# Block attention of a three-block model: rotated halves of q and k moved by transfers instead of matmuls, and one output piece placed before the last scores

## The reference, cut to what matters

```python
def apply_rope(t, cos, sin):
    t1, t2 = jnp.split(t, 2, axis=-1)
    return jnp.concatenate([t1 * cos - t2 * sin, t2 * cos + t1 * sin], axis=-1)

def moba_attention(x, w_qkv, w_o):
    qkv = (x @ w_qkv).reshape(B, T, 3, H, Dh)
    q, k, v = [jnp.transpose(qkv[:, :, n], (0, 2, 1, 3)).astype(f32) for n in range(3)]
    q = apply_rope(q, cos, sin) * (Dh ** -0.5)
    k = apply_rope(k, cos, sin)
    ...
    p = jax.nn.softmax(jnp.where(causal, q @ k.T, -jnp.inf), axis=-1)
    return (p @ v) @ w_o
```

## Time and profile before

| | |
|---|---|
| median of 3 runs | 1288.44 us (1288.23 to 1289.37) |
| the profiled execution | 1289.13 us, its span 1287.3 us |
| TensorE busy | 1240.8 us, 96% of the span |
| VectorE, ScalarE, GpSimd busy | 900.3, 640.5, 69.9 us |
| moved from and to HBM | 202.83 MB read, 158 GB/s over the span |

### The profile page before, as it was taken

How to read it: one execution, slowest core, us unless ns; L and a number is a source line. 1 busy time by engine, 2 the same in 40 slices (tenths; PEclk the granted TensorE clock), 3 DMA queues, 4 the chain that set the end, 5 groups by cost and what they waited for, 6 DMA issues and landing times.

```text
span 1287.3 us, 22080 instructions
## 1 busy us (share of the span) xinstructions
PE 1240.8 (96%) x9364; PEld 1086.4 (84%) x9364; DVE 900.3 (70%) x1433; ACT 640.5 (50%) x966; POOL 69.9 (5%) x43
## 2 busy tenths in 40 slices
PE   6999999999999999999999999999999999999997
PEld 4888898888888898778888889999898987788886
DVE  7456886767556677666765568989999766666555
ACT  3443446554445545555455545344455556655553
POOL 0022000002000061000100010000000000000000
PEclk8999999999999999999999999999999999999999
DMA  9442202775655373427565546455534443355550
GB/s 323 142 138 79 88 3 73 231 239 182 202 184 181 132 242 135 131 72 242 182 201 188 194 136 210 132 174 186 164 132 164 136 159 115 117 204 189 193 180 33
DMA packets 156355, 206.36 MB, mean 160 GB/s; under 512 B 9952, under 2 KB 129888, under 8 KB 156128
## 3 DMA queue, kind: packets, MB, share of 16 engines
q1 hardware_dynamic: 156256, 204.94, 48.3%
HBM read 202.83 MB, written 1.05 MB: 158 GB/s over the span
## 4 chain that ended last, share of the span: by engine, by line
PE 71%; DVE 19%; ACT 7%; issue 2%; DMA 0%; DVEq 0%; SPq 0%; ACTq 0%
PE PS L599 15%; PE PS L551 11%; PE PS L552 11%; PE PS L553 11%; PE PS L604 8%; DVE WW L2189 6%; PE PS L972 4%; DVE PH L2792 4%; ACT WW L1543 2%; PE PS L903 1%; DVE PA L2435 1%; ACT Xb L1582 1%; PE PS L943 1%; PE PS L676 1%; DVE PH L2810 1%
## 5 line engine op out<-in xcount | busy, mean ns | idle before, releaser
L2189 DVE TENSOR_TENSOR WW<-RG,WW 128x2048 fp32r<-128x2048 f32 x164 | 381.1, 2338 | 141.2 <-ACT WW L1543 141.0
L1543 ACT ACTIVATE WW<-RG 128x2048 fp32r<-128x2048 f32 x164 | 311.2, 1906 | 25.1 <-PE PS L553 24.5
L599 PE MATMUL PS<-AHL,WW 128*128 128x512 f32 x864 | 216.9, 392 | 0.5 <-DVE WW L2189 0.5
L551 PE MATMUL PS<-AHL,WW 128*128 128x256 f32 x704 | 203.3, 289 | 2.5 <-DVE AHL L2235 1.8
L552 PE MATMUL PS<-AHL,WW 128*128 128x256 f32 x704 | 199.1, 283 | 0.0
L553 PE MATMUL PS<-AHL,WW 128*128 128x256 f32 x704 | 199.1, 283 | 0.0
L599 PEld LDWEIGHTS PS<-AHL,WW 128*128 128x128 f32 x864 | 157.0, 189 | 30.0 <-DVE WW L2189 0.9
L551 PEld LDWEIGHTS PS<-AHL,WW 128*128 128x128 f32 x704 | 134.9, 192 | 5.3 <-issue 3.7
L552 PEld LDWEIGHTS PS<-AHL,WW 128*128 128x128 f32 x704 | 135.0, 192 | 1.7 <-issue 1.4
L553 PEld LDWEIGHTS PS<-AHL,WW 128*128 128x128 f32 x704 | 134.9, 192 | 0.0
L604 PEld LDWEIGHTS PS<-AHL,WW 128*128 128x128 f32 x864 | 118.4, 190 | 8.8
(11 more groups left out here) (375 smaller groups left out, 1829.0 us busy)
## 6 DMA issues: line engine op xcount, KB each, us to landing
RG<-in_ffn_w_in SPq DMA_DIRECT2D x44, 1024.0 KB, 5.3
RG<-in_w_ff SPq DMA_DIRECT2D x32, 1024.0 KB, 5.5
RG<-in_w_in SPq DMA_DIRECT2D x30, 1024.0 KB, 5.2
RG<-in_ffn_w_down SPq DMA_DIRECT2D x22, 1024.0 KB, 4.9
RG<-in_w_rkv SPq DMA_DIRECT2D x12, 1024.0 KB, 6.5
RG<-in_moba_w_qkv SPq DMA_DIRECT2D x12, 1024.0 KB, 6.5
RG<-in_w_o SPq DMA_DIRECT2D x4, 1024.0 KB, 7.9
RG<-in_wx_kv SPq DMA_DIRECT2D x4, 1024.0 KB, 5.4
```

The source lines that it names most:

```text
L551: e.matmul(o, lh, rh, start=start, stop=False)
L599: e.matmul(PS[b][:, :].rearrange("p (a t) -> p a t", a=2), wh, AHL[:, :, k * 256:k * 256 + 256], start=k == 0, stop=False)
L1543: s.activation(WH[hi_n % NW], ring(SPLIT[hi_n]), ACT.Copy, bias=0.0, scale=1.0).then_inc(s_hi, 1)
L2189: v.tensor_tensor(WL[lo_n % NW], ring(SPLIT[lo_n]), WH[lo_n % NW].bitcast(F32), ALU.subtract).then_inc(s_lo, 1)
```

## The change

The product with the permutation matrix is gone. In its place SP issues four transfers of 32 partitions by 512 columns (64 KB each) from `raw` to a new place `rot` in the tile `Xb`, swapped in pairs of 32 partitions (`rotate`). They stand in SP's list between the weights: `rotate(0)` behind mv3s, 1 behind mq3, 2 behind mk3s, 3 to 5 behind mo0 to mo2, 6 and 7 behind the first two pieces of the next feed-forward layer. The sign has moved into the table of sines. VectorE waits for the four transfers of a half (a count of 64 for each use) and reads `rot`. TensorE's waits before q and k pieces that write the PSUM banks again are now on `s_rw` instead of `s_rp`. Two waits are added on ScalarE. Lastly the output piece `moba_out(0, 1)` stands inside the step of heads 12 and 13, before their scores.

```diff
-               ('sel2', 2), ('pad', 14), ('perm', 128), ('cmask', 384), ('c01', 384), ('cos', 256), ('sin', 256)]:
+               ('sel2', 2), ('pad', 14), ('cmask', 384), ('c01', 384), ('cos', 256), ('sin', 256)]:
...
-    put('sin', np.tile(np.sin(ang), (4, 1)))
+    put('sin', np.where(p64 < 32, -1.0, 1.0) * np.tile(np.sin(ang), (4, 1)))
...
+        rot = [Xb[:, 1024 + 512 * n:1536 + 512 * n] for n in range(2)]
...
+            def rotate(u):
+
+                d.wait_ge(s_rw, u + 1)
+                for o_, i_ in ((0, 32), (32, 0), (64, 96), (96, 64)):
+                    d.dma_start(rot[u % 2][o_:o_ + 32, :], raw[u % 2][i_:i_ + 32, :]).then_inc(s_rot[u % 2], 16)
...
                             piece(f'f{f}{un}{j}', wcols(w_in, u * 256 * n + 256 * j, 256))
+                            if (f, j) == (1, 0):
+                                rotate(6 + u)
...
                     piece('mv3s', wcols(M, 2560, 512, 4, 4))
-                piece(f'mq{j}', wcols(M, 256 * j, 256))
-                piece(f'mk{j}s', wcols(M, 1024 + 256 * j, 256))
+                    rotate(0)
+                for u in range(2):
+                    piece(f'mk{j}s' if u else f'mq{j}', wcols(M, 1024 * u + 256 * j, 256))
+                    if j == 3:
+                        rotate(1 + u)
             for n in range(4):
                 piece(f'mo{n}', wcols(a['moba_w_o'], 512 * (n % 2), 512, 4 * (n // 2), 4))
+                if n < 3:
+                    rotate(3 + n)
...
                 if i in (12, 14):
+                    if between is not None:
+                        between()
                     e.wait_ge(s_rp, 8)
                     scores()
...
                     if u >= 4:
-                        e.wait_ge(s_rp, u - 3)
+                        e.wait_ge(s_rw, u - 3)
...
             moba_out(0, 0, (0, 1))
-            rope_turn(7)
+            e.wait_ge(s_rw, 8)
             moba_out(0, 0, (2, 3))
-            step()
-            moba_out(0, 1)
+            step(lambda: moba_out(0, 1))
...
+                if u == 0:
+                    s.wait_ge(s_tl, H_AT['ln1'] + 4)
                 s.activation(raw[u % 2], PS[4 + u % 4][:, :], ACT.Copy, bias=0.0, scale=1.0).then_inc(s_rw, 1)
...
             s.wait_ge(s_oa, 6)
+            s.wait_ge(s_rp, 8)
             rounded(OTf, (2,), 1.0, XH)
...
-                v.wait_ge(s_pm, u + 1)
-                own_dve(v.tensor_tensor(d_, PS[4 + u % 4][:, :].rearrange("p (m t) -> p m t", m=2), sinb, ALU.mult))
+                v.wait_ge(s_rot[u % 2], 64 * (u // 2) + 64)
+                own_dve(v.tensor_tensor(d_, rot[u % 2].rearrange("p (m t) -> p m t", m=2), sinb, ALU.mult))
```

More of the change, by code:

```diff
@@ L58, in constants @@
     put('sel2', (p // 64) == np.arange(2)[None, :])
-    n_out, n_in = f % 64, p % 64
-    same = (p // 64) == (f // 64)
-    put('perm', np.where(same & (n_out < 32) & (n_in == n_out + 32), -1.0, 0.0)
-        + np.where(same & (n_out >= 32) & (n_in == n_out - 32), 1.0, 0.0))
     t1 = np.arange(256)[None, :] - 128
@@ L214, in build @@
         s_fg, s_fx, s_fhh, s_fhl, s_dn = (sem(n) for n in ("ffn_gate", "ffn_prod", "ffn_hi", "ffn_lo", "ffn_down_mm"))
-        s_rw, s_rc, s_pm, s_rp, s_v2 = (sem(n) for n in ("rope_raw", "rope_cos", "rope_mm", "rope_out", "moba_v"))
+        s_rw, s_rc, s_rp, s_v2 = (sem(n) for n in ("rope_raw", "rope_cos", "rope_out", "moba_v"))
+        s_rot = [sem(f"rope_rotated{n}_in") for n in range(2)]
         s_sc, s_mx, s_ex, s_pn, s_pt, s_pta, s_pv, s_oa = (sem(n) for n in (
@@ L791, in attention, with attention_pairs @@
                     t.then_inc(s_pv, 1)
-            def attention_pairs(i):
+            def attention_pairs(i, between=None):
                 A = A1
@@ L1262, in tensor_program, with step @@
             mem_unit(3)
-            def rope_turn(u):
-                e.wait_ge(s_rw, u + 1)
-                e.matmul(PS[4 + u % 4][:, :], cst('perm'), raw[u % 2], start=True, stop=True).then_inc(s_pm, 1)
-            def step():
+            def step(between=None):
                 nonlocal heads
@@ L1272, in step @@
                     e.wait_ge(s_rp, heads // 2 + 2)
-                attention_pairs(heads)
+                attention_pairs(heads, between)
                 heads += 1
@@ L1287, in tensor_program @@
                     token_piece('mv3s', 6, 0, 1)
-                    rope_turn(5)
                     token_piece('mv3s', 7, 1, 1)
@@ L1305, in tensor_program @@
                         step()
-                        if u != 6:
-                            rope_turn(u - 1)
                     chan_piece(name, 4 + u % 4, 1)
@@ L1310, in tensor_program @@
                         step()
-                    elif u:
-                        rope_turn(u - 1)
             def moba_out(n, tt, ks=range(4)):
```

## The result

The changed kernel is slower. Four executions took 1299.12, 1299.17, 1300.71 and 6461.05 us. The last is an outlier that the comparison leaves out; the median of the other three, 1299.17 (1299.94 with it), stands for the kernel from here on. Runs of the kernel before beside them: 1288.84 (1288.23 to 1289.37). The ratio is 1.0083, with a 95% interval from 1.0070 to 1.0097. The forecast was 1295.0 with a range of 1287.5 to 1299.5: slower, as forecast, but by 10.3 us instead of 6.6. The one median lies just inside the range, the one of all four executions just outside.

The account below looks back on a forecast made before the run. It took TensorE as the bound, with VectorE close behind. Late rotations, carried through the loop and last heads, left the stage 6.65 us late; added to the median 1288.44 this gave 1295.0 us, range 1287.5 to 1299.5.

Parts of the forecast that it names:

- The queue: SP's full queue: transfers of rotations 0 and 1 stand behind 1 MB weights, landing at about 478.55 and 482.85.
- Rival B: SP's queue: small transfers do not queue behind the weights, rotation 1 is ready as before; 1287.7 us, chance 0.12.
- The sine product from SBUF: VectorE's product with the sines, reading SBUF instead of PSUM: 0.7 us taken against 0.68, no change.
- The clock: Behind TensorE's 7.7 us wait before the first score pair: half clock, mostly hidden; value 0.5 us, bounds 0 and 3.1.
- two waits of about 2 us: TensorE at the next two score pairs: waits about 2 us each, held by VectorE's and ScalarE's loop, 7.4 us late.
- The wait at the first output piece: TensorE's 1.17 us wait there grows by rotation 6's saved 0.85 us.
- First output piece: TensorE reaches it at 533.75 + 6.55 = 540.3, the 6.55 us lateness carried from the v pieces.
- Rotation 7 in at 543.55: Last rotation: raw half ready at 539.45, four transfers add 4.1 us; 7.3 us later than read before.
- head 12 to the last remainder 11.8: VectorE's last heads: between 10.6 and 13.0 us, 11.8 taken, against 12.97 before.
- Head 12 itself: VectorE's start on head 12, after TensorE's scores and the moved output piece: 548.3, 7.85 us later than 540.46.
- The end of the stage: End of mo3's remainder: 562.4 against 555.71, 6.65 us late, with nothing changed from there on.
- up to 2.6 more: Unknown size of the half-clock loss: up to 2.6 us beyond the value taken.

Follow-up runs that it names:

- 12: Changed kernel with rotations 0 to 2 earlier in SP's list, old output order, cosine product on VectorE, four filler matmuls: 1291.76 us, ratio 1.0023.
- 15: Changed kernel with rotations 0 to 5 re-placed in SP's list, old output order, cosine product on VectorE, four filler matmuls: 1287.73 us, ratio 0.9991.
- kernel 8: Changed kernel plus thirteen filler matmuls, results never read, in TensorE's waits, nine of them before the first score pair: 1297.82 us, ratio 1.0065.
- Experiment 4: Kernel before with the eight rotation matmuls left out and nothing in their place, so the result lacks the rotation: 1289.69 us, ratio 1.0005.
- kernel 5: Kernel before without any rotation, plus six filler matmuls, results never read, in TensorE's waits: 1287.15 us, ratio 0.9988.
- 13: Changed kernel with only SP's list changed, rotations 0 to 5 placed elsewhere among the weights: 1292.25 us, ratio 1.0021.
- 3: Kernel before with only the second output piece moved ahead of the scores of heads 12 and 13: 1289.98 us, ratio 1.0008.
- 14: Changed kernel with rotations 0 to 5 re-placed in SP's list, six filler matmuls and the old output order: 1288.86 us, ratio 1.0000.
- kernel 2: Changed kernel with halves 0 and 1 rotated by permutation matmul again, halves 2 to 7 by transfers: 1293.17 us, ratio 1.0032.
- kernel 10: Changed kernel with only rotations 0, 1 and 2 moved, to ahead of mq2, behind mk2s and behind mv2s: 1292.77 us, ratio 1.0030.
- 9: Changed kernel with halves 0 and 1 by matmul, rotation 2 ahead of mq3, six filler matmuls, old output order: 1288.03 us, ratio 0.9993.
- 6: Changed kernel with halves 0 and 1 by matmul and rotation 2 issued ahead of mq3 and mk3s: 1292.18 us, ratio 1.0023.
- 1: Changed kernel with SP's list reordered, rotation 0 ahead of mv2s and rotation 1 ahead of mv3s: 1296.31 us, ratio 1.0060.
- 7: Changed kernel with halves 0 and 1 by matmul, rotation 2 ahead of mq3 and mk3s, plus six filler matmuls: 1288.76 us, ratio 1.0001.
- 11: Changed kernel with rotations 0 to 2 earlier in SP's list, six filler matmuls and the old output order: 1292.66 us, ratio 1.0027.

## Why the prediction was right in direction and too small

All times here are those of the changed kernel plus 0.72, to stand beside before.

- **The queue: right.** Rotation 0 in at 479.2 (forecast 478.55), rotation 1 at 483.1 (482.85), landing 8.4 to 10.1 and 6.7 to 10.3 us after issue behind mv3s and mq3. Rival B's overtaking didn't come.
- **The sine product from SBUF, "I take 0.7, no change": wrong.** It took 1.39 us at rotation 1. With the 0.3 of the later landing the sum was ready at 485.3, not 484.3, and the first pair 7.0 late, not 6.0. The reason for the 0.7 is GpSimd's cosine product, below; without it (kernels 12 and 15) all eight sine products took 0.68 to 0.69. At the fifth pair 0.5 of this was left (7.0 late, forecast 6.55).
- **The clock, "value 0.5": too small by itself, and in the wrong place.** The forecast looked for it behind the first wait. There it was longer than taken (10.24 us, 5.12 of it over work) and hidden, as argued: of the two waits of about 2 us that were forecast for the pairs behind, the half clock used up the first (TensorE doesn't wait at the third pair) and left 1.61 of the second, where kernel 8 at full clock has 1.51 and 1.37. The forecast put nothing on a second window. The wait at the first output piece, which it made 1.17 + 0.85 = 2.0 us long itself, came out at 3.13, 1.07 of it by VectorE's remainder, with the clock at half for 3.42 behind it. From that piece to head 12 it cost 1.45 (9.47 us instead of 8.0); kernel 8, without the window, is 1.38 faster there.
- **First output piece: 541.9 instead of 540.3.** 0.5 is the rest from the first pair, 1.07 that VectorE's 512-column remainder stood still beside GpSimd's product. The forecast had "6.55 late" carried to this piece unchanged.
- **Rotation 7 in at 543.55, head 12 to the last remainder 11.8: right** (read at 543.7; 11.67). Head 12 itself 551.3 against 548.3: 0.5 + 1.07 + 1.45.
- **The end of the stage: 9.58 late, not 6.65**, the same 3.0 less rounding. Then 1.04 lost behind it and 0.72 won ahead, where half-clock windows in unchanged code differ.

So the path of the forecast held (queue, VectorE, first pair, last heads), and the failed step is two of its terms. The clock was valued at 0.5 behind the first wait and at nothing behind the output piece's, where it cost 1.45. VectorE's instructions were taken at their old length ("I take 0.7, no change"), where GpSimd's product cost 1.07 at the output piece and most of 0.5 at the first pair. With 0.3 of windows outside the stage these are the 3.3 us between the forecast for the profiled execution, 1295.8, and the measured 1299.12. The 1.07 is partly bad luck: which of VectorE's two remainders meets GpSimd's product is a matter of some hundredths of a microsecond (last section). The forecast's own bound, "up to 2.6 more" for the clock, covers the clock alone.

What the forecast and its rivals all had wrong is the other side of the ledger. They priced TensorE's saved 6.8 us between 0.8 and 6.8. Experiment 4 puts them at nothing, -0.9 by the medians with an interval that holds 0 (ratio 1.0005, 0.9997 to 1.0014): the time goes into waits behind the loop of VectorE and ScalarE, which was forecast; behind the waits the clock is at half (3.27 us of the stage by kernel 5), and VectorE's remainder falls beside GpSimd's product (1.1), which weren't. Splitting the stage's 9.58 by the experiments: 5.94 is the place of transfers in the queue (changed against 13), 0.87 the output piece (3), 3.17 the clock (13 against 14, 4.04 less 0.87), and -0.40 is all that transfers in place of matmuls give when these are gone (14 against before). In the -0.40, 1.0 lost at VectorE's remainder is still contained.

## What to carry to other kernels

Small transfers placed in the queue of large prefetches inherit their latency, and moving one ahead pushes the next behind: check each landing against its reader, not only the one that was late. Before taking work off the busiest engine, ask which wait it will turn into; on TensorE idle stretches of 2 to 3 us were in most cases followed by 3.4 us at half clock, so that 6.8 us of work removed made this kernel no faster (its stage 1.5 us longer), and useless products in the waits gained 2.5 to 3.4 us. VectorE's time for an instruction with both inputs from SBUF depended on what GpSimd did in the same microsecond (0.69 or up to 1.79 us).

## What the hardware did that was not expected

**Half clock behind short waits.** In the stage of kernel 4, waits of 2.31 and 3.13 us were each followed by the granted clock at 0.5, 1.2 GHz, for 3.4 us; the 1.61 us wait of the changed kernel was not, nor were kernel 2's of 3.14 and kernel 10's of 3.12. The kernel before shows it behind 3.05 us already. Which waits it follows is therefore not settled by their length, and was not tried further. The Trainium skill (TensorE: Matmul & The Clock Gate, "HAM oscillation — how this bites in real kernels") describes waits between bursts of matmuls after which each burst starts at the lower clock, and prices it at half the time spent there. By that rule, as an estimate, kernel 13's two windows cost (3.41 + 3.42) / 2 = 3.4 us; its stage against kernel 14's says 3.17 and kernel 4's against kernel 5's 3.27, so the runs agree.

**Windows in unchanged code.** Near 780 us, where TensorE waits twice, 1.1 to 1.8 us each, the clock was at half for 6.8 us in the profiled executions of the changed kernel and of 3, 10, 12 and 14, for 3.4 in 5 and 9, and not at all in the others. From the layer norm behind the stage to the transposes near 1053 us it takes 486.5 to 486.6 us without, 487.0 with 3.4 and 487.4 to 487.5 with 6.8. The window near 24 us also differs: 6.8 us in before, 6, 8 and 14, none in 2, 3 and 5, 3.4 in the others. The two may be much of the 2 us by which executions of one kernel differ; only one execution of each was profiled, so this is not shown.

**VectorE beside GpSimd.** GpSimd's cosine product and VectorE's sine product in the changed kernel (the latter, with both inputs from SBUF, is shown above: it took 1.39 us from 482.43 and ended 0.5 us behind GpSimd's):

```profile
480.72 2.56 POOL L2996 TENSOR_TENSOR PH<-PH,CB 128x512 f32<-128x512 f32 x1 [10.56 <-ACT PH L1959]
```

In the kernel before, the product with one input from PSUM, inside GpSimd's time:

```profile
475.39 1.30 POOL L2991 TENSOR_TENSOR PH<-PH,CB 128x512 f32<-128x512 f32 x1 [4.51 <-ACT PH L1955]
475.57 0.69 DVE L2720 TENSOR_TENSOR PH<-PS,CB 128x512 f32<-128x512 f32 x1 [1.95 <-PE PS L1267]
```

It took its usual 0.69. At the first output piece, the kernel before and then the changed kernel:

```profile
532.92 2.38 DVE L2729 TENSOR_TENSOR ML<-PH,XH 128x512 fp32r<-128x512 f32 x2
532.96 1.79 POOL L2991 TENSOR_TENSOR PH<-PH,CB 128x512 f32<-128x512 f32 x1 [6.12 <-ACT PH L1955]
```

```profile
539.19 1.27 POOL L2996 TENSOR_TENSOR PH<-PH,CB 128x512 f32<-128x512 f32 x1 [6.06 <-ACT PH L1959]
539.22 2.38 DVE L2734 TENSOR_TENSOR ML<-PH,XH 128x512 fp32r<-128x512 f32 x2
```

Before, GpSimd's product began 0.04 us behind VectorE's first remainder, and the first was fast (0.69) and the second slow (1.78); in the changed kernel it began 0.03 us ahead, the first took 1.78, and TensorE waited for just that one. Kernels 1 and 3 have the order of before; 2, 4 to 11, 13 and 14 that of the changed kernel, kernel 4 with no transfer in it at all; in 12 and 15 both remainders took 0.68. The Trainium skill (SBUF — State Buffer, "Who interferes with whom") says that a VectorE instruction with two inputs from SBUF and a GpSimd instruction that reads SBUF exclude each other, and that the one that starts second stands still. The trace agrees on all three. At the sine product it is a rule that spoke against the change, since it took the PSUM input away, and the forecast hadn't weighed it; at the output piece the inputs are the same as before, and only the order of the two starts has turned.

**The last of four.** Behind or between weights the fourth of a rotation's transfers at times landed well behind the third: in kernel 6 the four of rotation 2 took 2.1 to 4.0 us, the last being the 4.0, and landed at 478.54 (the third) and 481.11; in the changed kernel rotation 2 shows 1.8 us between the two, rotations 0 and 1 only 0.4 and 0.3. On a free queue they follow each other by 0.6 to 0.7. Why was not tried.
